# Hybrid RWKV-7 and attention block on one core: both levels of the block inverse on 32x32 tiles of TensorE, with strips of 64 columns for X and XT and the R and O products between their steps; final squares in two parts

## The chip, the core and the metric

The kernel runs on one core of a Trainium2 chip. The metric is the device time of one execution in microseconds (us); lower is better. PE is TensorE (PEld its weight loads), DVE is VectorE, ACT ScalarE, POOL GpSimd, and SP the engine whose queue starts the DMAs. T = 1024 tokens, model width 1024, all in float32 (F32R for the operands of the dense products).

## The reference, cut to what matters

One layer of a streaming encoder: norm, one input projection, an RWKV-7 head group (8 heads of 64) beside a sliding-window attention group, an output projection, a SwiGLU FFN, a final norm. The change touches the recurrence of the RWKV group and the final norm:

```python
def step(S, inp):
    r_t, w_t, k_t, v_t, kk_t, a_t = inp
    sa = jnp.einsum('bhvk,bhk->bhv', S, -kk_t)
    S = (S * w_t[:, :, None, :]
         + sa[..., None] * (kk_t * a_t)[:, :, None, :]
         + v_t[..., None] * k_t[:, :, None, :])
    return S, jnp.einsum('bhvk,bhk->bhv', S, r_t)
...
def rmsnorm(x, g):
    xf = x.astype(jnp.float32)
    y = xf * lax.rsqrt(jnp.mean(xf * xf, axis=-1, keepdims=True) + NORM_EPS)
    return (y * g.astype(jnp.float32)).astype(x.dtype)
```

## The kernel before, in words

The program is written out in eight stages; in each, every engine has a function of its own, and semaphores tie them together. Stages 1 to 3 (to 355 us) do the input projection, the attention and the inputs of the recurrence. Stage 5 (about 355 to 574 us) is the recurrence, stages 6 and 7 (to about 1082 us) are the output projection and the gate and up products, stage 8 is the down product and the final norm.

**The recurrence** takes the tokens in eight turns (`for t in range(NT)`) of 128. Within a turn the sequential rule is solved in matrices: for each of the 8 heads a 128x128 strictly triangular matrix (kept transposed in NB, two buffers by the parity of t), whose unit-triangular inverse is needed in its two 64x64 diagonal blocks. The inverse is made in three levels:

- `lanes(t)` on DVE (line 1613) inverts all 64 diagonal blocks of 16x16 (8 a head) with one partition for each. Its way in and out goes through DRAM: `gather` (1326) writes NB to `n_scratch` and reads the 16x16 blocks into LA; `scatter` (1340) writes the results (LM) to `inv_scratch` and reads them back as X (the inverse) and XT (its transpose), 128 partitions by 8 heads by 128 columns, with zeros where no block stands.
- Level 1 joins two blocks of 16 to one of 32, level 2 two of 32 to one of 64. On PE each level is `corners(n, t)` (NB times X, 1410) and `updates(n, t)` (the masked result Ts times XT, 1419), in two halves of four heads, each a product of 128x128 a head. DVE's `corners` (1599) multiplies by a mask of the constants and writes Ts1 or Ts2; DVE's `updates` (1607) adds the result to XT. Between the levels PE transposes XT (`transposed`, 1404) and ACT copies it to X.

**The order is written by hand.** Each engine runs its list in program order. PE in a turn: first corners, first updates, `outputs(t-1)` (transposes of the last turn's result, 1433), transposes for X, `cumulative(t+2)` (decay sums, 1254), second corners and updates, R (lines 1475 to 1480), the first part of O (1485), U, and the rest, ending in `following(t+1)`. DVE in a turn: corners, `normalise(t-1)` (1666), updates, `outputs(t-1)`, second corners and updates, `prepare(t+2)` (1291, four operations with ACT's exponentials of the decay sums), `lanes(t+1)`, masks of KB (1321), Sn (1720), means of the output, more masks of KB and, for turn t+2, of NB. ACT's exponentials (1277) come before its copy of R. PSUM has eight banks; `order5` (1221) lists the jobs in the order in which they take their banks, and a job waits for the one before it in its bank.

**The final norm** (stage 8): the last unit of the down product (m = 27) gives the block c21. `by_tokens` (2349) transposes it to tokens: its first three column blocks just before the unit's last two k steps, the fourth behind it. ACT squares 512 columns a token tile with a row sum (`square`, 2428); DVE adds the sums, ACT takes the root, both scale, and SP writes out.

## Time and profile before

| | |
|---|---|
| median of 3 runs | 1327.61 us (1326.69 to 1328.05) |
| profiled execution, its own time | 1324.93 us |
| its span, first to last instruction | 1323.0 us |
| granted TensorE clock, mean | 0.994 |
| busy: PE, PEld | 1275.8 us (96%), 1057.7 us (80%) |
| busy: DVE, ACT, POOL | 853.1 us (64%), 479.3 us (36%), 254.3 us (19%) |
| DMA | 179.05 MB, mean 135 GB/s |

The profiled execution is 2.7 us below the median. Busy times overlap and are averages over stages with different limits: the 96% of PE tell nothing of where a change on another engine would be felt. A matmul record ends when its result is out, so neighbouring records overlap; the distance between starts is what one costs in a stream.

### The profile page before, as it was taken

What the parts mean: (1) busy time and instruction counts of PE and PEld (TensorE: products, weight loads), DVE (VectorE), ACT (ScalarE), POOL (GpSimd) and SP (SyncE); (2) the same over time, 40 slices, a digit from 0 to 9 for tenths busy, and PEclk for the clock granted to TensorE, in tenths of its full rate; (3) what the DMA queues carried; (4) which work ended last, traced back from release to release, by engine and by line L of the source; (5) the groups of instructions that cost most, each with busy time, mean ns of one, the idle gap of its engine ahead of it and who ended that gap; (6) DMA issues with size and microseconds to landing.
All of it is one profiled execution on the core that took longest, in us unless ns stands there. A gap on an engine that the chain in (4) does not pass through costs nothing.

```text
span 1323.0 us, 18110 instructions
## 1 busy us (share of the span) xinstructions
PE 1275.8 (96%) x6973; PEld 1057.7 (80%) x6973; DVE 853.1 (64%) x1308; ACT 479.3 (36%) x847; POOL 254.3 (19%) x196
## 2 busy tenths in 40 slices
PE   7999999989899999999999999999999999999996
PEld 6888888655698888888878888888888888888885
DVE  6865623399778787744476656566777676546765
ACT  6100032488422232234363333333333334333334
POOL 0476600034300000000003331332233200000001
PEclk9999999999999999989999999999999999999998
DMA  5576532200322333333214123214544567766643
GB/s 222 173 246 232 207 121 92 104 2 17 80 71 71 75 103 94 115 123 127 80 48 127 52 93 96 83 62 159 175 141 162 191 222 293 250 210 209 210 140 135
DMA packets 117232, 179.05 MB, mean 135 GB/s; under 512 B 30368, under 2 KB 59040, under 8 KB 116896
## 3 DMA queue, kind: packets, MB, share of 16 engines
q1 hardware_dynamic: 117152, 177.96, 41.0%
q8 instruction: 53, 0.87, 0.3%
q14 instruction: 27, 0.22, 0.0%
HBM read 123.90 MB, written 53.49 MB: 134 GB/s over the span
## 4 chain that ended last, share of the span: by engine, by line
PE 88%; DVE 7%; issue 2%; DMA 2%; ACT 2%; POOL 0%; DVEq 0%; SPq 0%; ACTq 0%; POOLq 0%
PE bank L2317 28%; PE bank L369 21%; PE bank L2417 15%; PE bank L1400 4%; PE bank L474 2%; PE bank L383 2%; PE bank L1271 1%; PE bank L1527 1%; PE bank L1485 1%; PE bank L1479 1%; DVE scores L1178 1%; PE bank L992 1%; PE bank L1497 1%; PE bank L1514 1%; PE bank L1501 1%
## 5 line engine op out<-in xcount | busy, mean ns | idle before, releaser
L2317 PE MATMUL bank<-thi,ahi 128*128 128x512 f32 x320 | 124.5, 389 | 0.0
L2317 PE MATMUL bank<-tlo,ahi 128*128 128x512 f32 x320 | 124.5, 389 | 0.0
L2317 PE MATMUL bank<-thi,alo 128*128 128x512 f32 x320 | 124.5, 389 | 0.0
L2417 PE MATMUL bank<-ch,dwh 128*128 128x512 f32 x308 | 120.3, 391 | 0.6 <-DVE dwl L1995 0.6
L2417 PE MATMUL bank<-ch,dwl 128*128 128x512 f32 x308 | 119.9, 389 | 0.0
L2417 PE MATMUL bank<-cl,dwh 128*128 128x512 f32 x308 | 119.8, 389 | 0.0
L348 DVE TENSOR_TENSOR ring_wlo<-ring_raw,ring_whi 128x1024 fp32r<-128x1024 f32 x30 | 40.6, 1352 | 121.9 <-ACT ring_whi L342 121.9
L369 PE MATMUL bank<-hhi,ring_whi 128*128 128x512 f32 x288 | 114.4, 397 | 0.0
L369 PE MATMUL bank<-hhi,ring_wlo 128*128 128x512 f32 x288 | 112.2, 390 | 0.0
L369 PE MATMUL bank<-hlo,ring_whi 128*128 128x512 f32 x288 | 112.1, 389 | 0.0
L2317 PE MATMUL bank<-x1hi,ahi 128*128 128x512 f32 x240 | 93.4, 389 | 0.0
L2317 PE MATMUL bank<-x1lo,ahi 128*128 128x512 f32 x240 | 93.4, 389 | 0.0
L2317 PE MATMUL bank<-x1hi,alo 128*128 128x512 f32 x240 | 93.4, 389 | 0.0
L342 ACT ACTIVATE ring_whi<-ring_raw 128x1024 fp32r<-128x1024 f32 x30 | 31.6, 1057 | 153.8 <-PE bank L369 142.2
L1991 ACT ACTIVATE dwh<-dwr 128x1408 fp32r<-128x1408 f32 x28 | 38.7, 1382 | 112.7 <-PE bank L2417 108.1
L2317 PEld LDWEIGHTS bank<-thi,alo 128*128 128x128 f32 x320 | 60.1, 188 | 12.6
L2317 PEld LDWEIGHTS bank<-thi,ahi 128*128 128x128 f32 x320 | 60.1, 188 | 12.5
L2317 PEld LDWEIGHTS bank<-tlo,ahi 128*128 128x128 f32 x320 | 60.1, 188 | 12.4
L2417 PEld LDWEIGHTS bank<-ch,dwh 128*128 128x128 f32 x308 | 57.8, 188 | 12.9 <-DVE dwl L1995 1.0
L2417 PEld LDWEIGHTS bank<-ch,dwl 128*128 128x128 f32 x308 | 57.8, 188 | 12.1
L2417 PEld LDWEIGHTS bank<-cl,dwh 128*128 128x128 f32 x308 | 57.8, 188 | 11.8
L369 PEld LDWEIGHTS bank<-hhi,ring_whi 128*128 128x128 f32 x288 | 54.1, 188 | 11.9 <-issue 1.0
(336 smaller groups left out, 2862.2 us busy)
## 6 DMA issues: line engine op xcount, KB each, us to landing
hraw<-hid_scratch SPq DMA_DIRECT2D x12, 1024.0 KB, 5.7
hid_scratch<-hid SPq DMA_DIRECT2D x22, 512.0 KB, 6.1
hid_scratch<-rt SPq DMA_DIRECT2D x11, 1024.0 KB, 4.7
dwr<-down_sums SPq DMA_DIRECT2D x16, 704.0 KB, 4.2
ring_raw<-in_w_in SPq DMA_DIRECT2D x20, 512.0 KB, 4.3
raw_a<-in_w_gate_up SPq DMA_DIRECT2D x20, 512.0 KB, 4.4
raw_b<-in_w_gate_up SPq DMA_DIRECT2D x20, 512.0 KB, 5.2
dwr<-in_w_down SPq DMA_DIRECT2D x12, 704.0 KB, 4.1
```

The lines of the kernel that those rows point to most:

```text
L342: act.activation(self.ring.hi[:, s, 0:self.kt, :], self.ring.raw[:, s, 0:self.kt, :], ACT.Copy).then_inc(self.ring.hi_ready, 1)
L348: dve.tensor_tensor(self.ring.lo[:, s, 0:self.kt, :], self.ring.raw[:, s, 0:self.kt, :], self.ring.hi[:, s, 0:self.kt, :].bitcast(F32), AL ...
L369: mm = pe.matmul(o[:, :], wpart[:, s, k, :], apart[:, k, c], start=i == 0, stop=i == n - 1)
L383: mm = pe.matmul(bank[self.J.bank_of[f"{s}{half}"]][:, :], wpart[:, s, ks[n], :], apart[:, ks[n], c], start=n == 0 and i == 0, stop=n == l ...
L474: mm = pe.matmul(b[:, :], wpart[:, s, k, :], apart[:, k, c], start=k == 0 and i == 0, stop=k == KD - 1 and i == 2)
L992: mm = pe.matmul(bank[6][HD * e:HD * e + HD, p * P:(p + 1) * P], vt[:, t + j, (p // 2) * HD:(p // 2 + 1) * HD], pt[:, p % 2, j, e, :], sta ...
L1178: ins = dve.tensor_tensor_reduce(sc[:, h, c0:BAND], b[:, i * BAND + c0:(i + 1) * BAND], bias[:, h, c0:BAND], HD ** -0.5, snk[:, h:h + 1], ...
L1271: mm = pe.matmul(b[e][:, i * 2 * P:(i + 1) * 2 * P].rearrange("p (a n) -> p a n", a=2), src[r, 2 * g + i, tok(t)], rho_alpha(t, r, 2 * g + ...
L1400: mm = pe.matmul(b[:, j * P:(j + 1) * P], lhs(4 * g + j), rhs(4 * g + j), start=j == 0, stop=j == 3, skip_group_check=True)
L1991: act.activation(dw_hi[m % 2][:, :, :], dw_raw[m % 2][:, :, :], ACT.Copy).then_inc(ring2.hi_ready, 1)
L2317: mm = pe.matmul(b[:, :], w[:, k, :], m[:, k, :], start=opens and k == 0 and i == 0, stop=not (j, n) in parts and k == 3 and i == 2, skip_ ...
L2417: mm = pe.matmul(b[:, :], w[m % 2][:, k, :], a[:, k, :], start=opens and k == 0 and i == 0, stop=name not in PART2 and k == KF - 1 and i = ...
```

## The change

Per turn of the recurrence:

- Both levels of the inverse are computed on 32x32 tiles: `blocks_of` goes over the 8 heads and, for each, over four tiles (first corners with 16 columns, first updates with 32) or over two (the second level, and a new product for X that takes the place of the transposes). Each job fills one bank instead of two.
- X and XT keep 64 columns a head, the diagonal 64x64 blocks alone. Each is loaded in two transfers of 64 partitions, so that `scatter` issues five DMAs instead of three.
- On DVE the first corners are one `tensor_scalar` by a column of the constants, the first updates one add to X and one to XT, the last update two copies. ACT, which no longer copies X, copies Ts2.
- The order changes. On PE `outputs(t-1)` stands between the first corners and the first updates; the second corners stand behind R, the second updates behind O, and the decay sums for t+2 behind those. ACT takes its exponentials behind R and Ts2.
- The masks of the two levels (256 columns) leave the constants.

In stage 8 the first three column blocks of the last block are transposed two k steps earlier (at k = 7 instead of k = 9, of 0 to 10), ACT squares these 384 columns beside the last products, and only 128 columns a tile are left for the end; DVE adds the extra sums.

```diff
         for t in range(NT):
-            order5 += [("t10", t, 0), ("t11", t, 6), ("y10", t, 4), ("y11", t, 5)]
+            order5 += [("t1", t, 0), ("y1", t, 4), ("x1", t, 6)]
             order5 += [("ot", t - 1, 7)] if t else []
-            order5 += [("x10", t, 2), ("x11", t, 3)] + plan_cum(t + 2)
-            order5 += [("t20", t, 0), ("t21", t, 6), ("y20", t, 4), ("y21", t, 5)]
-            order5 += [("R", t, 0), ("O", t, 5), ("U", t, 2)]
+            order5 += [("R", t, 0), ("t2", t, 2), ("O", t, 5), ("y2", t, 4)] + plan_cum(t + 2) + [("U", t, 2)]
...
-                sp.dma_start(X[:, :, :], bass.AP(d_i.tensor, P, [[2 * P, P], [8 * IMG2, H], [1, P]])).then_inc(s_xl, 16)
-                if t:
-                    C.result(sp, "U", t - 1)
-                sp.dma_start(XT[:, :, :], bass.AP(d_i.tensor, 0, [[2 * P, P], [8 * IMG2, H], [1, P]])).then_inc(s_xt, 16)
+                for m, o, done in ((X, P, s_xl), (XT, 0, s_xt)):
+                    if t and m is XT:
+                        C.result(sp, "U", t - 1)
+                    for q in range(2):
+                        sp.dma_start(m[q * HD:(q + 1) * HD, :, :],
+                                     bass.AP(d_i.tensor, o + q * (2 * P + 1) * HD, [[2 * P, HD], [8 * IMG2, H], [1, HD]])
+                                     ).then_inc(done, 16)
...
+            def blocks_of(b, count, lhs, rhs, groups):
+                n = len(groups) * H
+                for h in range(H):
+                    for g in groups:
+                        lo, ro = lhs(g, h), rhs(g, h)
+                        to = g[2]
+                        mm = pe.matmul(b[32 * to:32 * to + 32, h * count:(h + 1) * count] if len(ro.shape) == 2 else
+                                       b[32 * to:32 * to + 32, h * count:(h + 1) * count].rearrange("p (a w) -> p a w", a=2),
+                                       lo, ro, start=h == 0, stop=h == H - 1, skip_group_check=True)
+                return mm
+            FOUR = [(g, g % 2, g) for g in range(4)]
             def corners(n, t):
+                if n == 1:
+                    b = C.claim(pe, "t1", t)
+                    pe.wait_ge(s_xl, 32 * t + 32)
+                    C.done(blocks_of(b, 16, lambda g, h: NB[t % 2][rows(g[0]), h, 1, rows(g[0])],
+                                     lambda g, h: X[rows(g[0]), h, 32 * g[1]:32 * g[1] + 16], FOUR), "t1", t)
+                else:
+                    b = C.claim(pe, "t2", t)
+                    C.emptied(pe, "x1", t)
+                    C.done(blocks_of(b, 32, lambda g, h: NB[t % 2][rows(g[0]), h, 1, rows(g[2])],
+                                     lambda g, h: X[rows(g[0]), h, 0:32], [(0, 0, 1), (2, 0, 3)]), "t2", t)
...
                 corners(1, t)
-                pe.wait_ge(s_xt, 16 * t + 16)
-                updates(1, t)
                 if t:
                     outputs(t - 1)
-                for g in range(2):
-                    C.emptied(pe, f"y1{g}", t)
-                    transposed("x1", g, t)
-                if t + 2 < NT:
-                    cumulative(pe, t + 2)
-                corners(2, t)
-                updates(2, t)
+                pe.wait_ge(s_xt, 32 * t + 32)
+                updates(1, t)
...
                 mm.then_inc(s_r, 1)
+                corners(2, t)
...
+                updates(2, t)
+                if t + 2 < NT:
+                    cumulative(pe, t + 2)
...
+            def first_corners(t):
+                b = C.result(dve, "t1", t)[:, 0:16 * H].rearrange("p (h n) -> p h n", h=H)
+                C.read(dve.tensor_scalar(Ts1[:, :, 0:16], b, cst[:, C_PAIR + 2:C_PAIR + 3], None, ALU.mult), "t1", t)
+            def first_updates(t):
...
+                C.read(dve.tensor_tensor(X[:, :, 0:16], c, X[:, :, 0:16], ALU.add), "x1", t)
+                C.read(dve.tensor_tensor(v, b, v, ALU.add), "y1", t)
+            def last_updates(t):
...
+                dve.tensor_copy(XT[0:32, :, 32:64], b[0:32, :, :])
+                C.read(dve.tensor_copy(XT[64:96, :, 32:64], b[64:96, :, :]), "y2", t)
...
-                    if m == 4 * len(TURN) - 1 and k == KF - 2:
+                    if m == 4 * len(TURN) - 1 and k == 7:
                         by_tokens(pe, 0, 1, 0, 3)
...
+            def square_three(n):
+                act.wait_ge(s_part, len(parts) + 12 + n + 1)
+                act.activation(fin[:, n, HALF:HALF + 3 * P], D2.bank("f01", n)[:, 0:3 * P], ACT.Square,
+                               accum_out=st[:, 4, n:n + 1]).then_inc(s_sq8, 1)
+            def square_last(n):
+                b = D2.result(act, "f01", n)
+                act.activation(fin[:, n, HALF + 3 * P:D], b[:, 3 * P:HALF], ACT.Square, accum_out=st[:, 1, n:n + 1]
+                               ).then_inc(s_sq8, 1)
```

How the order moves on PE in one middle turn. In these rows Ts_90 is Ts1 and Ts_91 is Ts2, `cst,sgt` are the decay sums, `S,arv` with the first `vtk,KB` is R, and the second `vtk,KB` is O. Before:

```order
L1400 MATMUL bank<-X,NB_89 128x128 x8
L1400 MATMUL bank<-XT,Ts_90 128x128 x8
L1437 MATMUL bank<-cst,on 128x128 x4
L1407 MATMUL bank<-cst,XT 128x128 x8
L1259 MATMUL bank<-cst,sgt 128x129 x4
L1400 MATMUL bank<-X,NB_89 128x128 x8
L1400 MATMUL bank<-XT,Ts_91 128x128 x8
L1476 MATMUL bank<-S,arv 128x128 x4
L1479 MATMUL bank<-vtk,KB 128x64 x8
L1485 MATMUL bank<-vtk,KB 128x64 x8
L1493 MATMUL bank<-rs,XT 64x64 x8
```

The same stretch of PE's list, from the first corners to U, in the changed kernel:

```order
L1406 MATMUL bank<-X,NB_89 32x16 x32
L1455 MATMUL bank<-cst,on 128x128 x4
L1406 MATMUL bank<-XT,Ts_90 32x32 x32
L1406 MATMUL bank<-Ts_90,XT 32x16 x16
L1487 MATMUL bank<-S,arv 128x128 x4
L1490 MATMUL bank<-vtk,KB 128x64 x8
L1406 MATMUL bank<-X,NB_89 32x32 x16
L1497 MATMUL bank<-vtk,KB 128x64 x8
L1406 MATMUL bank<-XT,Ts_91 32x32 x16
L1251 MATMUL bank<-cst,sgt 128x129 x4
L1507 MATMUL bank<-rs,XT 64x64 x8
```

The last update of the inverse (`XT,Ts_91`) has moved from ahead of R to behind O, and the decay sums from ahead of the second level to the last place before U.

On ACT, the same turn; `rs` is the copy of R, `ein` to `einv` the exponentials of the decay sums, which `prepare` on DVE reads. Before:

```order
L1547 ACTIVATE X<-bank 128x512 x2
L1284 ACTIVATE ein<-bank 128x258
L1285 ACTIVATE ecs<-bank 128x2
L1287 ACTIVATE ems<-bank 128x2
L1288 ACTIVATE einv<-bank 128x256
L1284 ACTIVATE ein<-bank 128x258
L1285 ACTIVATE ecs<-bank 128x2
L1287 ACTIVATE ems<-bank 128x2
L1288 ACTIVATE einv<-bank 128x256
L1570 ACTIVATE rs<-bank 64x512
L1572 ACTIVATE us<-bank 64x512
```

And in the changed kernel:

```order
L1576 ACTIVATE rs<-bank 64x512
L1561 ACTIVATE Ts_91<-bank 128x256
L1276 ACTIVATE ein<-bank 128x258
L1277 ACTIVATE ecs<-bank 128x2
L1279 ACTIVATE ems<-bank 128x2
L1280 ACTIVATE einv<-bank 128x256
L1276 ACTIVATE ein<-bank 128x258
L1277 ACTIVATE ecs<-bank 128x2
L1279 ACTIVATE ems<-bank 128x2
L1280 ACTIVATE einv<-bank 128x256
L1581 ACTIVATE us<-bank 64x512
```

The exponentials have moved behind the copy of R.

## Rows read from the trace of the kernel before

**Rows 1.** The page's fourth part: chain that ended last, shares of the span by engine.

```profile
PE 88%; DVE 7%; issue 2%; DMA 2%; ACT 2%; POOL 0%; DVEq 0%; SPq 0%; ACTq 0%; POOLq 0%
```

**Rows 2.** Chain of waits, whole span: start us, us, what.

```profile
468.33 1.16 PE bank L1400 x8
...
496.69 1.16 PE bank L1400 x8
```

**Rows 3.** Timeline of one turn, PE: start us, us, engine line op out<-in xcount [idle before].

```profile
466.98 1.13 PE L1400 MATMUL bank<-X,NB 128*128 128x128 f32 x8 [0.29 <-DMA X<-inv_scratch]
...
471.76 0.60 PE L1437 MATMUL bank<-cst,on 128*128 128x128 f32 x4
...
473.07 1.06 PE L1259 MATMUL bank<-cst,sgt 128*128 128x129 f32 x8
...
477.54 1.06 PE L1476 MATMUL bank<-S,arv 128*128 128x128 f32 x8
...
478.43 1.90 PE L1479 MATMUL bank<-vtk,KB 128*128 128x64 f32 x16
...
480.17 1.95 PE L1485 MATMUL bank<-vtk,KB 128*128 128x64 f32 x16
...
482.05 1.14 PE L1493 MATMUL bank<-rs,XT 64*64 64x64 f32 x16
...
495.26 1.02 PE L1400 MATMUL bank<-X,NB 128*128 128x128 f32 x7 [0.19 <-DMA X<-inv_scratch]
```

**Rows 4.** Timeline of the same turn, DVE, ACT and SP's queue.

```profile
466.94 2.56 DVE L1321 COPY_PREDICATED NB<-cst,bank 128x512 f32<-128x512 uint32 x4
...
470.06 0.67 DVE L1668 TENSOR_TENSOR on<-oc,sm 128x512 f32<-128x512 f32 x1
...
473.81 0.39 ACT L1284 ACTIVATE ein<-bank 128x258 f32<-128x258 f32 x1
...
474.81 0.48 ACT L1288 ACTIVATE einv<-bank 128x256 f32<-128x256 f32 x1
...
478.08 0.68 DVE L1297 TENSOR_TENSOR ab<-ab,einv 128x512 f32<-128x512 f32 x1
...
480.56 0.15 DVE L1640 TENSOR_TENSOR LM<-LA 64x8 f32<-64x8 f32 x1
...
487.80 0.58 SPq L1344 DMA_DIRECT2D inv_scratch<-LM  x1
...
488.71 1.35 DVE L1321 COPY_PREDICATED KB<-cst,bank 128x512 f32<-128x512 uint32 x2 [0.94 <-PE bank L1271]
...
491.09 0.38 SPq L1351 DMA_DIRECT2D X<-inv_scratch  x1
```

**Rows 5.** DMA issues in the recurrence: out<-in queue op xcount, KB each, median us to landing.

```profile
LA<-n_scratch SPq DMA_DIRECT2D x7, 64.0 KB, 2.7
```

**Rows 6.** Groups by line and shape, PE: busy us, mean ns of one, idle before.

```profile
L992 PE MATMUL bank<-pt,vt 128*64 128x128 f32 x256 | 21.3, 285 | 1.1
...
L1493 PE MATMUL bank<-rs,XT 64*64 64x64 f32 x128 | 9.1, 221 | 0.0
```

**Rows 7.** Timeline of the attention stage, PE.

```profile
328.45 0.66 PE L992 MATMUL bank<-pt,vt 128*64 128x128 f32 x8
```

**Rows 8.** Stretches: PE, PEld, DVE, ACT, POOL busy us, granted clock, DMA share, GB/s.

```profile
440.00:468.00 28.00, 27.29 (x252) 25.40 (x252) 21.94 (x49) 7.82 (x21) 1.46 (x3) 1.00 0.32 79
...
569.90:573.30 3.40, 2.85 (x14) 2.85 (x14) 1.78 (x2) 3.38 (x4) 0.00 (x0) 0.50 0.00 0
```

**Rows 9.** Timeline of the last turn, PE, around the drop of the clock.

```profile
568.63 1.14 PE L1514 MATMUL bank<-rs,XT 64*64 64x64 f32 x16 [0.68 <-ACT rs L1547]
...
570.46 3.67 PE L1527 MATMUL bank<-us,NB 128*128 128x64 f32 x16 [0.68 <-ACT us L1547]
```

**Rows 10.** Timeline of the last turn's head (DVE) and of the kernel's end (ACT).

```profile
553.81 0.69 DVE L1668 TENSOR_TENSOR on<-oc,sm 128x512 f32<-128x512 f32 x1 [1.49 <-POOL sm L1395]
...
1312.83 0.60 ACT L2431 ACTIVATE fin<-bank 128x512 f32<-128x512 f32 x1 [7.23 <-PE bank L2355]
```

More of the change, by code:

```diff
@@ L58, in constants @@
     c[:, C_LID:C_LID + 256:17] = 1
-    def corner(b):
-        return (s // (2 * b) == t // (2 * b)) & (s % (2 * b) >= b) & (t % (2 * b) < b)
-    for n, b in enumerate(LEVELS):
-        c[:, C_LEV + n * P:C_LEV + (n + 1) * P] = corner(b)
     c[:, C_BLK:C_BLK + P] = s // HD == t // HD
@@ L1419, in updates @@
-            def updates(n, t):
-                m = Ts1 if n == 1 else Ts2
-                for g in range(2):
-                    C.emptied(pe, f"t{n}{g}", t)
-                    b = C.claim(pe, f"y{n}{g}", t)
-                    C.done(four(b, g, lambda h: m[:, h, :], lambda h: XT[:, h, :]), f"y{n}{g}", t)
+            def blocks_of(b, count, lhs, rhs, groups):
[8 more added lines that the diff above has]
+                return mm
@@ new lines, in updates @@
+            def updates(n, t):
+                C.emptied(pe, f"t{n}", t)
+                if n == 1:
+                    b = C.claim(pe, "y1", t)
+                    C.done(blocks_of(b, 32, lambda g, h: Ts1[rows(g[0]), h, :],
+                                     lambda g, h: XT[rows(g[0]), h, :].rearrange("p (a w) -> p a w", a=2)[:, :, 16:32], FOUR),
+                           "y1", t)
+                    b = C.claim(pe, "x1", t)
+                    C.done(blocks_of(b, 16, lambda g, h: XT[rows(g[0]), h, 0:32],
+                                     lambda g, h: Ts1[rows(g[0]), h, 0:16], [(0, 0, 0), (2, 0, 2)]), "x1", t)
+                else:
+                    C.emptied(pe, "y1", t)
+                    b = C.claim(pe, "y2", t)
+                    C.done(blocks_of(b, 32, lambda g, h: Ts2[rows(g[0]), h, :],
+                                     lambda g, h: XT[rows(g[0]), h, 32:64], [(1, 0, 0), (3, 0, 2)]), "y2", t)
@@ L1513, in stage5_tensor @@
                 for h in range(H):
[L1514 removed]
+                    mm = pe.matmul(bu[high, h * HD:(h + 1) * HD], XT[high, h, :], rs_[high, h * HD:(h + 1) * HD],
                                    start=h == 0, stop=h == H - 1, skip_group_check=True)
@@ L1543, in stage5_scalar, with keep @@
             low, high = slice(0, HD), slice(HD, P)
-            def keep(job, t, dst, rows=slice(0, P)):
+            def keep(job, t, dst, rows=slice(0, P), cols=HALF):
                 b = C.result(act, job, t)
-                C.read(act.activation(dst, b[rows, :], ACT.Copy), job, t)
-            def keep_x(job, t):
-                for g in range(2):
-                    keep(f"{job}{g}", t, row(X[:, 4 * g:4 * g + 4, :]))
+                C.read(act.activation(dst, b[rows, 0:cols], ACT.Copy), job, t)
             def tokens(t):
@@ L1561, in stage5_scalar @@
                     mix_high(act, 0)
-                keep_x("x1", t)
-                if last:
+                    C.result(act, "x1", t)
                     mix_high(act, 1)
-                if t + 2 < NT:
-                    exponentials(act, t + 2, 0, 1)
-                if last:
                     mix_high(act, 2)
@@ L1570, in stage5_scalar @@
                 act.activation(rs_[low, :], bank[0][low, :], ACT.Copy).then_inc(s_rlow, 1)
+                keep("t2", t, row(Ts2[:, :, :]), cols=32 * H)
+                if t + 2 < NT:
+                    exponentials(act, t + 2, 0, 1)
                 act.wait_ge(s_u, t + 1)
@@ L1692, in stage5_vector @@
                 last = t == NT - 1
-                corners(1, t)
+                first_corners(t)
                 if t:
                     normalise(t - 1)
-                updates(1, t)
+                first_updates(t)
                 if t:
@@ L1700, in stage5_vector @@
                     mix_low(dve, 0)
-                corners(2, t)
-                if last:
                     mix_low(dve, 1)
-                updates(2, t)
+                last_updates(t)
                 if not last:
@@ L2353, in by_tokens @@
                 b = D2.bank(f"f{half}{g}", n) if first else D2.claim(pe, f"f{half}{g}", n)
+                if first:
+                    pe.wait_ge(s_sq8, 12 + n + 1)
                 for q in range(first, end):
@@ L2459, in stage8_scalar @@
                     first_columns(0)
+                    for n in range(4):
+                        square_three(n)
             for n in range(3):
-                square(0, 1, n)
+                square_last(n)
             root(1)
-            square(0, 1, 3)
+            square_last(3)
             first_columns(1)
@@ L2557, in stage8_vector @@
                 combine(m)
+            dve.wait_ge(s_sq8, 16)
+            order(dve.tensor_tensor(st[:, 0, 0:4], st[:, 0, 0:4], st[:, 4, 0:4], ALU.add))
             total(1)
```

59 lines of the change are left out of this document (19 added, 40 removed).

## The prediction

> **What bounds the kernel now.** I read first the chain of waits over the whole span: PE carries 88% of it [rows 1], most of it in dense products that the change leaves alone. The change lies in the recurrence (stage 5, about 355 to 574 us) and in the last 15 us. In the recurrence the same group of the chain comes back at 468.33 and 496.69 [rows 2]: a turn takes 28.36 us, and seven such steps separate the eight turns. A reader could stop here and call PE the bound, since it is busy 27.29 of 28.00 us there [rows 8]. But the timeline shows what PE waits for at the head of a turn: the last thing before the first corner products is the landing of X, with 0.29 us idle at 466.98 and 0.19 at 495.26 [rows 3]. Following X back through the timeline of the other engines [rows 4] gives a ring as long as the turn:
>
> - head (466.98) to the start of `prepare` on DVE (478.08): 11.10 us. DVE stands in program order: `prepare` follows the last update of XT.
> - `prepare` to the start of `lanes` (480.56): 2.48 us.
> - `lanes` to the issue of the scatter (487.80): 7.24 us.
> - scatter to the issue of X (491.09): 3.29 us; X to the next head (495.26): 4.17 us.
>
> The sum is 28.28 us. So two bounds lie on each other: PE's own work and the ring head, last update, `prepare`, `lanes`, scatter, X. Less work on PE is worth nothing unless "head to `prepare`" becomes shorter as well.
>
> **The change, part by part.**
>
> *Products of the inverse.* A turn loses 40 products of 128x128, which the trace counts as 80 instructions (two for each), and gains 112 products on 32x32 tiles, 224 instructions. The old price is 111 ns for an instruction: the 8 of L1476 start at 477.54 and L1479 follows at 478.43 [rows 3]. The new one is in no row, so I bound it. One 64x64 tile at a time: 16 instructions in 1.14 us, one lasting 0.221, so (1.14-0.221)/15 = 61 ns [rows 3, 6]; with half the columns 31 ns, the upper end. If two independent tiles overlap fully, the rate doubles: L992 alternates two column tiles and does 8 instructions of 128 columns in 0.66 us, (0.66-0.285)/7 = 54 ns, half of 111 [rows 6, 7]. Four tiles would make 31/4 = 8 ns, the lower end. Of the 224, 128 go to four tiles and 96 to two: (128x8+96x16)/224 = 11 ns. I take 13, near the lower end, because the row that is nearest shows full overlap: 2.9 us a turn instead of 8.9, between 1.8 and 6.9.
>
> *Changes of tile shape.* Each of the four tile groups now stands between wide products, also new. The nearest rows are wide to 64x64 and back: L1485 starts at 480.17, its 16 instructions at 111 ns end at 481.95 and L1493 starts at 482.05, 0.1 us later [rows 3]. I take 0.2 to 0.3 us for there and back, 1.1 us a turn. The Trainium skill (TensorEngine Tiling (Array Packing), Key Properties) says that changing the tiling mode drains the engine, and these 0.1 us agree.
>
> *The instruction floor.* The same page (Instruction Overhead) says that each matmul has some 60 cycles of overhead, so that one of a few columns costs as much as one of 60. By that page a step would be an estimated 25 ns, 5.6 us a turn, and the sum below would be about 22 us higher. It speaks against this change, and is a rival below, priced from rows.
>
> *The order on PE.* This is what I weigh most. Before, the second corners and updates ran ahead of R, and the decay sums for t+2 (L1259) ran early, so that ACT's exponentials were done at 475.29, long before `prepare` [rows 4]. Now the last update comes behind R and O, and the sums behind that, and behind those ACT's exponentials. Head to `prepare`, with 13 ns an instruction:
> corners 64x13 + 0.2 = 1.0; DVE's Ts1 and two handovers 0.6; DVE's `normalise` 0.67 and its handover 0.15, since `outputs` now stands ahead of the first updates on PE and waits for it [rows 4]: 2.4. `outputs`, 4 instructions (L1437) at 0.11 [rows 3]: 2.8. First updates 96x13 + 0.3: 4.4. R, 477.54 to 480.17, 2.6 [rows 3]: 7.0. Second corners 32x13 + 0.3: 7.7. O, 480.17 to 482.05, 1.9: 9.6. Second updates 0.7: 10.3. Decay sums and exponentials, 473.07 to 475.29, 2.2 [rows 3, 4]: 12.6 us, against 11.1. DVE's last update and ACT's copy of Ts2 cost nothing: they lie beside the sums and beside O.
>
> *X in strips.* X goes from one transfer of 512 KB (4.17 us) to two of 128 KB. Bounds: LA's 64 KB takes 2.7 us [rows 5], and nothing excludes that two issues and 256-byte pieces eat the gain. I take 3.6, so -0.5 a turn. XT has four issues' time more on SP, but is needed only after `outputs`.
>
> *The rest of the ring* (`prepare` on, 17.2 us) is unchanged. So a turn is longer by 1.5-0.5 = 1.0 us, seven times: +7. DVE loses eight and gains five short operations, but it was late nowhere in the ring; its tail behind `lanes` (masks, Sn, the head's means, masks; L1321 at 488.71 waits 0.94 us today [rows 4]) takes up the wait and ends about when X lands. PE then waits some 4 us for DVE's Sn, which frees the bank of `kt`: late next, and hidden under the ring.
>
> *Last turn.* No ring follows it, so here PE's saving counts: 80x0.111 = 8.9 less 2.9 and 1.1 is 4.9, of which the wait for POOL's power before `normalise`, 1.49 us [rows 10], stays: -3.3. Together +3.7 us at full clock.
>
> *Clock.* The profile shows the granted clock at 1.00 (2.4 GHz) through the whole recurrence but for one place: at 569.9 to 573.3 it is 0.50 (1.2 GHz) [rows 8]. What PE did just before was 64x64 products (L1514) with a wait of 0.68 us on either side, nothing wide [rows 9]; 16 instructions of L1527 then took 3.67 us, where 16 of the same shape take 1.90 (L1479) [rows 3, 9]. In the changed turn PE does, around the head, a wait, small tiles, a wait for `normalise`, four wide instructions and small tiles again: over 5 us with less wide work than before that drop. I expect the drop there in most turns. R follows: 24 instructions at (3.67-1.90)/16 = 0.11 us more each are +2.6 us on the ring. In 6 of 8 turns: +15.7 us.
>
> *Split squares.* Three fourths of the columns of four squares move under the last products. Of each of ACT's squares of 0.60 us on the last stretch [rows 10] about 0.25 goes, three of them on the path: -0.8 (between -1.1 and 0). The shorter constants load no later than before; I cost them at nothing, under the input's own loads.
>
> **The sum.** 3.7 + 15.7 - 0.8 = +18.6 us on the profiled execution's 1324.93 us: 1343.5. The median of the runs, 1327.61, is 2.7 above that execution, so I say 1346.
>
> **Rivals.**
>
> 1. *Small tiles are dearer*: one tile at a time, 31 ns, or a floor for each instruction. For it: no row shows four tiles or 16 columns. Against it: L992's full overlap. 31-13 = 18 ns on 224 instructions is 4.0 us a turn, 32 in eight: 1378; with the clock kept 1362; at half that excess with the drop 1362.
>
> 2. *The clock holds*, the pace as I take it. For it: a turn of today keeps 1.00 with three groups of 64x64 products and the waits at its head in it [rows 8]. 1346-15.7 = 1330.
>
> 3. *Faster*: the clock holds and four tiles run side by side at 8 ns. Place: the first updates behind `normalise`. 160 instructions on the ring 5 ns cheaper are -0.8 a turn, which with the strips of X landing in 3.1 us makes the turn 28.1 and the sum of the seven about -2, the last turn -4.4, the squares -0.8: 1320 to 1324. It decides when head to `prepare` falls below 11.1 us plus what X gains; at 13 ns it is 1.0 us over.
>
> **How the numbers follow.** Forecast (tiles near 8 to 16 ns, clock drops) 0.43, 1335 to 1355. Rival 1 0.27, 1355 to 1380. Rival 2 0.13, 1327 to 1334, half of it within 0.2%. Rival 3 0.14. An unseen slack in the ring that favours the change 0.03. About 0.2% (2.7 us) is what a measurement of this kernel can tell from no change. Faster 0.17, same 0.08, slower 0.75. The range leaves out the fast end of rival 3 and the dear end of rival 1: 1322 to 1374.
>
> **What would show it.** Right: turns of 30 to 32 us; `prepare` starting 12.5 us or more after the head, released by ACT's exponentials and not by the last update; `outputs` on PE waiting for `normalise`; granted clock 0.50 in most turns with R at twice its length; a new wait of PE for Sn. Wrong: small tiles over 20 ns an instruction in a stream (rival 1), PEclk 1.00 throughout (rival 2), or turns under 28.4 us, in which case the ring was not the bound that I make it.

## The result, and the profile after

The changed kernel takes 1406.05 us (median of 4 runs, 1390.90 to 1413.21) beside 1327.36 of the kernel before: 1.0555 times as long, interval 1.0472 to 1.0637. That is 79 us more, where I forecast 19. A ratio leaves out runs far above a kernel's fastest, so that of a kernel with a wide spread lies below the ratio of its medians. The profiled execution took 1413.21 us, the slowest of the four and 88.3 more than that of before; the rows below are its own.

Nearly the whole loss lies in the recurrence: from the first corners of turn 0 to the output projection it takes 306.6 us (354.20 to 660.81) instead of 219.2 (354.76 to 573.93), 87.4 of the 88.3 more. The page's clock line shows where to look:

```profile
PEclk9999999999655555555999999999999999999998
```

The stretches view of a middle turn, and of its parts at either clock (columns as in [rows 8]):

```profile
470.10:511.03 40.93, 37.83 (x406) 34.37 (x404) 20.87 (x47) 7.32 (x20) 1.83 (x2) 0.58 0.19 45
...
474.44:508.58 34.14, 34.14 (x318) 31.43 (x318) 15.68 (x37) 6.11 (x18) 0.00 (x0) 0.50 0.19 41
508.58:515.40 6.82, 3.72 (x92) 2.94 (x88) 5.19 (x9) 1.21 (x3) 1.83 (x2) 1.00 0.18 65
```

A turn is 40.93 us where it was 28.36 [rows 2], and for 34.14 of them the granted clock is 0.50 (1.2 GHz), with PE busy in all 34.14. In before it was 1.00 (2.4 GHz) throughout such a turn [rows 8]. PE's timeline of the same turn, to be held against [rows 3]:

```profile
476.32 2.08 PE L1487 MATMUL bank<-S,arv 128*128 128x128 f32 x8
478.18 3.51 PE L1490 MATMUL bank<-vtk,KB 128*128 128x64 f32 x16
481.63 1.06 PE L1406 MATMUL bank<-X,NB 32*32 32x32 f32 x32
482.62 3.67 PE L1497 MATMUL bank<-vtk,KB 128*128 128x64 f32 x16
486.23 1.06 PE L1406 MATMUL bank<-XT,Ts 32*32 32x32 f32 x32
487.22 2.09 PE L1251 MATMUL bank<-cst,sgt 128*128 128x129 f32 x8
...
511.03 0.73 PE L1406 MATMUL bank<-X,NB 32*32 32x16 f32 x64
514.86 0.63 PE L1455 MATMUL bank<-cst,on 128*128 128x128 f32 x4 [3.10 <-DVE on L1674]
```

R takes 5.31 us (476.32 to 481.63) instead of 2.63. The small tiles are not what is dear: the second corners take 0.99 us (481.63 to 482.62) and the second updates as much. The one wait left at the head is 3.10 us for `normalise`; it lies inside the stretch at 1.00, and the clock falls right behind it. DVE and ACT in that turn, beside [rows 4]:

```profile
489.73 0.40 ACT L1280 ACTIVATE einv<-bank 128x256 f32<-128x256 f32 x1
490.25 0.69 DVE L1289 TENSOR_TENSOR ab<-ab,einv 128x512 f32<-128x512 f32 x1 [2.06 <-ACT einv L1280]
...
511.35 2.53 DVE L1313 COPY_PREDICATED NB<-cst,bank 128x512 f32<-128x512 uint32 x4
513.78 0.34 DVE L1605 TENSOR_SCALAR Ts<-bank,cst 128x128 f32<-128x128 f32 x1
514.03 0.68 DVE L1674 TENSOR_TENSOR on<-oc,sm 128x512 f32<-128x512 f32 x1
```

As forecast, ACT's exponentials now release `prepare`. `normalise` is late because Ts1 and it stand behind DVE's masks of NB, which end 2.85 us after the head (511.03 to 513.88); the prediction had put their end at about the landing of X. `outputs` starts 3.83 us after the head, where its list has 2.4.

### The profile page after: what moved, and what is told of

Read it like the earlier page. It is cut to its first block, busy times and chain, and to the rows that moved or that the text cites. A ratio compares the mean times of both kernels' runs of the same rounds, so it can differ in the third digit from the quotient of the medians.

```text
span 1411.3 us, 20489 instructions
## 1 busy us (share of the span) xinstructions
PE 1345.7 (95%) x8189; PEld 1117.1 (79%) x8189; DVE 841.3 (60%) x1285; ACT 475.5 (34%) x847; POOL 254.0 (18%) x196
## 4 chain that ended last, share of the span: by engine, by line
PE 86%; DVE 7%; DMA 3%; ACT 2%; issue 2%; SPq 0%; POOL 0%; DVEq 0%; ACTq 0%; POOLq 0%
PE bank L2321 26%; PE bank L363 19%; PE bank L2425 13%; PE bank L1406 2%; PE bank L1497 2%; PE bank L1490 2%; PE bank L1263 2%; PE bank L468 2%; PE bank L377 2%; PE bank L1541 2%; DVE NB L1313 1%; PE bank L1511 1%; PE bank L1528 1%; PE bank L1507 1%; PE bank L1487 1%
## 5 line engine op out<-in xcount | busy, mean ns | idle before, releaser
L363 PEld LDWEIGHTS bank<-hlo,ring_whi 128*128 128x128 f32 x288 | 54.1, 188 | 12.0 <-issue 1.0
```

Of the source, the lines that this page charges most:

```text
L363: mm = pe.matmul(o[:, :], wpart[:, s, k, :], apart[:, k, c], start=i == 0, stop=i == n - 1)
```

## The experiments

All kernels, in the order of their runs; each ratio is to the kernel before as it ran beside them, with medians of 1325.6 to 1326.5. The last two columns are one stretch of the profiled execution, from the first R to the output projection, and its granted clock; for the changed kernel 303.3 us at 0.59, for the kernel before 209.9 at 0.99.

| kernel | median us (range) | ratio (interval) | stretch us | clock |
|---|---|---|---|---|
| squares | 1325.97 (1324.2-1328.1) | 0.9995 (0.9984-1.0007) | 209.9 | 1.00 |
| outputs back | 1368.97 (1364.5-1376.4) | 1.0322 (1.0273-1.0370) | 260.1 | 0.72 |
| fill | 1358.07 (1343.2-1370.0) | 1.0167 (1.0115-1.0219) | 250.7 | 0.80 |
| old order | 1384.35 (1375.8-1387.5) | 1.0417 (1.0377-1.0457) | 273.3 | 0.64 |
| fill three | 1358.86 (1345.5-1363.2) | 1.0218 (1.0164-1.0272) | 254.4 | 0.81 |
| lanes first | 1395.59 (1394.0-1409.1) | 1.0561 (1.0507-1.0616) | 286.3 | 0.61 |
| lanes, strips | 1334.01 (1321.3-1359.3) | 1.0036 (1.0005-1.0067) | 224.0 | 0.80 |
| wide, outputs | 1336.71 (1334.7-1339.8) | 1.0089 (1.0070-1.0107) | 221.2 | 0.98 |
| reordered | 1355.18 (1353.5-1361.5) | 1.0217 (1.0200-1.0233) | 246.3 | 0.72 |
| reordered, fill | 1353.72 (1349.5-1361.2) | 1.0213 (1.0186-1.0240) | 243.1 | 0.75 |
| corners on ACT | 1334.31 (1319.3-1355.1) | 1.0020 (0.9988-1.0052) | 222.9 | 0.80 |
| strips, fill | 1316.60 (1313.8-1323.3) | 0.9930 (0.9908-0.9952) | 209.0 | 0.89 |
| corners on ACT, fill | 1320.08 (1312.8-1343.7) | 0.9914 (0.9894-0.9934) | 212.1 | 0.89 |
| fill elsewhere | 1330.24 (1327.0-1348.4) | 1.0056 (1.0024-1.0089) | 220.1 | 0.86 |
| fewer products | 1309.73 (1307.8-1312.9) | 0.9873 (0.9851-0.9894) | 196.7 | 0.92 |
| last turns | 1316.90 (1305.7-1321.3) | 0.9894 (0.9858-0.9931) | 213.7 | 0.90 |

**Squares**: the kernel before with the hunks of stage 8 from the diff above, and nothing else.

> The kernel before with the change of the last stage alone (three fourths of four squares beside the last products). My term for it was -0.8 us, between -1.1 and 0: 1326.5 against 1327.4. If the squares are part of the loss, this kernel is slower than before by a microsecond or more. The recurrence must read as before: turns of 28.4 us, granted clock 1.00.

The end is shorter: from the last transposes to the last scaling 3.57 us (1316.16 to 1319.73) instead of 4.61 (1312.46 to 1317.07). Of the total, -0.7 us stays within its uncertainty. The squares are no part of the loss.

**Outputs back**, the changed kernel with one job of PE moved:

```diff
                 corners(1, t)
-                if t:
-                    outputs(t - 1)
                 pe.wait_ge(s_xt, 32 * t + 32)
                 updates(1, t)
+                if t:
+                    outputs(t - 1)
```

> The changed kernel with the transposes of the last turn's result put back behind the first updates, so that PE goes from the first corners to the first updates with DVE's Ts1 alone between them. Theory A (the granted clock falls because PE has next to nothing wide to do at the head of a turn: small tiles and a wait): the wait for normalise is only moved by 160 small instructions, so the clock still falls and the time stays at 1390 to 1410. Theory B (it is that one wait of 3.1 us between first corners and first updates on the way to the ring's last update): with it gone the clock holds in most turns and the time comes to 1330 to 1350.

Neither number: 37 us came back, and the clock still fell in every turn, for 3.4 to 7 us at a time in most and for 37 and 68 us twice. The wait matters but is not the whole cause. With `outputs` moved PE waits elsewhere, 3.3 us for Sn among others.

**Fill**, the changed kernel with products that nobody reads, each into a bank that the next job overwrites:

```diff
+            def filler(b, count):
+                for i in range(count):
+                    pe.transpose(b[:, i % 4 * P:i % 4 * P + P], ident, ident)
...
                     b = C.claim(pe, "t1", t)
+                    filler(b, 12 if t else 0)
...
                 b = C.claim(pe, "ot", t)
+                filler(b, 8 if t < NT - 1 else 0)
```

> The changed kernel with 20 extra transposes of 128x128 a turn, whose result nobody reads: 12 ahead of the wait for X and 8 ahead of the wait for normalise, about 4.4 us of PE at 2.4 GHz. It adds work and takes none away. Theory A (waits and small tiles at the head let the granted clock fall, and the low clock is the whole loss): granted clock 1.00 through the recurrence, turns of 28 to 31 us, 1325 to 1350 us. Theory C (the small tiles themselves cost more than an instruction of their size, or lower the clock whatever stands beside them): the clock still falls in every turn, turns of 41 us or more, 1400 to 1440 us.

More work made it 48 us faster, and its granted clock is 0.80 where the changed kernel has 0.59: most of the loss is the clock's. In the trace a transpose is one instruction; the first 12 took 1.46 us (457.55 to 459.01), so that 20 add some 2.4 us a turn and not the 4.4 that I gave. The later expectations price them too dear in the same way. It missed my 1350 by 8 us, and the timeline of PE (then one row of DVE) shows why:

```profile
451.66 1.12 PE L1453 MATMUL bank<-cst,arv 128*128 128x128 f32 x4 [3.31 <-DVE Sn L1730]
...
457.55 1.53 PE L1418 MATMUL bank<-cst 128*128 128x128 f32 x12
459.01 0.73 PE L1406 MATMUL bank<-X,NB 32*32 32x16 f32 x64
459.67 1.09 PE L1418 MATMUL bank<-cst 128*128 128x128 f32 x8
...
461.39 0.72 PE L1406 MATMUL bank<-XT,Ts 32*32 32x32 f32 x62
461.94 0.18 PE L1406 MATMUL bank<-Ts,XT 32*32 32x16 f32 x1
...
462.55 1.27 PE L1493 MATMUL bank<-S,arv 128*128 128x128 f32 x8
...
470.99 0.69 DVE L1289 TENSOR_TENSOR ab<-ab,einv 128x512 f32<-128x512 f32 x1 [1.37 <-ACT einv L1280]
```

Its stretches:

```profile
450.08:456.90 6.82, 5.24 (x24) 4.14 (x26) 5.04 (x11) 3.00 (x7) 0.00 (x0) 0.50 0.45 87
456.90:480.80 23.90, 22.60 (x404) 20.18 (x400) 15.41 (x37) 4.23 (x13) 1.83 (x2) 1.00 0.19 52
```

The head now keeps 1.00. In five of the turns the clock falls at the wait of 3.31 us for Sn, which I had named as late next, or just behind it.

**Old order**: small tiles kept, the order of before.

```diff
                 updates(1, t)
+                if t:
+                    outputs(t - 1)
+                if t + 2 < NT:
+                    cumulative(pe, t + 2)
+                corners(2, t)
+                updates(2, t)
...
                 mm.then_inc(s_r, 1)
-                corners(2, t)
```

> The changed kernel's small tiles in the order of before: outputs, decay sums, second corners and second updates ahead of R, exponentials ahead of the copy of R. Theory A: all 224 small instructions and their handovers to DVE and ACT now stand together at the head, with still less wide work between them, so the clock falls as before in every turn: 1385 to 1415. If the new order is what costs (theory D), the clock holds, turns are 26 to 28.5 us and the time 1310 to 1330.

One us under theory A's range, and far from D. Putting the order back does not put the time back. This kernel has no wait for `normalise` at its head; it waits up to 2.5 us for Ts1 instead.

**Fill three**: the fill also ahead of the wait for Sn.

```diff
                     b = C.claim(pe, kind, t)
+                    filler(b, 14 if kind == "bt" and t else 0)
```

> With 20 extra transposes the clock still fell for 6.8 us of every turn, right behind a wait of 3.3 us of PE for DVE's Sn. This kernel has extra transposes ahead of all three waits: 14 ahead of the kt transposes that wait for Sn, 8 ahead of X, 8 ahead of normalise, about 6.7 us of extra PE work a turn. Theory A (each stretch of waiting or of small tiles lets the clock fall, wherever in the turn it stands): granted clock 1.00 through the middle turns, turns of 29 to 30.5 us, set by the ring through DVE, 1330 to 1345 us. Theory C (the small tiles lower the clock whatever stands beside them): it falls in every turn as before, 1358 us or more.

The median missed theory A's range and is the number that I gave for theory C, but the clock did not fall in every turn as C has it: one of five middle turns has 27 us at 0.50, the other four hold 1.00 and take 29.0 to 30.3 us, as expected. The shortest of them:

```profile
424.30:453.30 29.00, 26.41 (x437) 23.60 (x436) 20.72 (x47) 7.22 (x20) 1.83 (x2) 1.00 0.26 62
```

In the next turn PE stands for 1.05 us within the first updates, with no releaser in the profile, and the clock is then 0.50 for 27 us. A turn of this order at full clock, with the fill in its waits, is thus 29.0 to 30.3 us: the order, the tiles and the strips together cost 0.6 to 1.9 us a turn, and the other 10.6 to 11.9 of the changed kernel's 40.93 are the clock's.

**Lanes first**, to take waits away instead of filling them: `lanes(t+1)` ahead of `prepare(t+2)`, and ACT instead of DVE copies the last update.

```diff
-                last_updates(t)
...
-                    if t + 2 < NT:
-                        prepare(dve, t + 2)
                     lanes(t + 1)
+                    if t + 2 < NT:
+                        prepare(dve, t + 2)
```

> The changed kernel with lanes(t+1) ahead of prepare(t+2) on DVE, and the last update of XT copied by ACT, so that DVE needs nothing of PE between outputs(t-1) and prepare. No extra work. The waits of PE for Sn (3.3 us) and for X should go, only that for normalise stays. Theory A: with less waiting PE keeps its clock in most turns, turns of 26.5 to 29 us, 1310 to 1335 us. If the one wait for normalise beside the small tiles of the head is enough for the clock to fall, it is low again in most turns: 1370 to 1400 us.

The second branch: with the 3.10 us for `normalise` left, the ratio (1.0561) is that of the changed kernel.

**Lanes, strips**: that, with `outputs` back as above, and the following (three changes at once, so their shares are not known):

```diff
-                sp.dma_start(bass.AP(d_n.tensor, 0, [[P, P], [8 * IMG, H], [1, P]]), NB[t % 2][:, :, 1, :]
-                             ).then_inc(s_img, 16)
+                for q in range(2):
+                    sp.dma_start(bass.AP(d_n.tensor, q * (P + 1) * HD, [[P, HD], [8 * IMG, H], [1, HD]]),
+                                 NB[t % 2][q * HD:(q + 1) * HD, :, 1, q * HD:(q + 1) * HD]).then_inc(s_img, 16)
```

> As the kernel with lanes first, and with outputs(t-1) behind the first updates on PE and n_scratch written from the 64 columns of each head's diagonal blocks alone (two transfers of 128 KB in place of one of 512 KB), which brings LA forward by about 1.5 us. Of the turn's waits only that for Ts1 is left. Theory A: granted clock near 1.00, turns of 25 to 27.5 us, 1300 to 1325 us, faster than both kernels. Theory C: the clock falls all the same, 1350 us or more.

A middle turn, and the last one:

```profile
415.50:441.40 25.90, 22.62 (x406) 20.32 (x404) 20.37 (x46) 7.86 (x22) 1.84 (x2) 1.00 0.22 45
551.06:581.40 30.34, 25.92 (x342) 24.64 (x340) 10.54 (x14) 9.83 (x14) 1.83 (x2) 0.50 0.17 63
```

The turn of 25.90 us was hit; the time was not, because the clock fell for 27 us in turn 0 and for 51 from the end of turn 6. At three heads between it fell for 3.4 us only, at one for 7. The fastest of ten runs, 1321.3, already beats the kernel before.

**Wide, outputs**: the kernel before with `outputs(t - 1)` moved ahead of the first updates.

> The kernel before, wide products and all, with one move of the change: outputs(t-1) on PE between the first corners and the first updates. PE then waits about 2 to 2.6 us for normalise at the head of each turn, and the ring is longer by 0.7 to 1.5 us a turn: 1333 to 1338 us if the clock holds. Theory A in its simple form (a wait of that length at the head is enough) says that the clock falls in most turns too and the time is 1350 us or more; if it holds at 1.00, the wait alone is not enough and the missing wide work of the inverse is needed as well.

```profile
363.60:560.40 196.80, 181.99 (x1666) 166.80 (x1664) 146.59 (x327) 51.42 (x128) 12.87 (x14) 1.00 0.32 84
```

The clock holds although PE waits there (0.25, 0.26 and 1.40 us at one head); turns are 29.6 us, 1.2 more than before. Beside wide products waits of this length do no harm; the wait for `normalise` is 1.40 us here and 3.10 in the changed kernel, so that this run doesn't try a wait as long as that one.

**Reordered**, and the same with fill:

```diff
-            order5 += [("t1", t, 0), ("y1", t, 4), ("x1", t, 6)]
+            order5 += [("t1", t, 0), ("y1", t, 3), ("x1", t, 1)]
...
+                C.read(act.activation(Ts1[:, :, 0:16], b, ACT.Copy, scale=cst[:, C_PAIR + 2:C_PAIR + 3]), "t1", t)
...
+                if t + 2 < NT:
+                    cumulative(pe, t + 2)
                 pe.wait_ge(s_vtk, 16 * t + 16)
```

> The kernel with lanes first and strips, whose middle turns are 25.8 to 26.4 us at the full clock and wait 2.5 us for Ts1 behind DVE's masks of NB. Here ACT makes Ts1, y1 and x1 take banks that the masks do not hold, the decay sums stand within R so that prepare runs while DVE waits for LA, and vtk is loaded ahead of XT. No extra work. Theory A: the last long wait of PE in a middle turn is gone, turns of 24 to 25.5 us with the granted clock at 1.00, 1295 to 1320 us, the rest lost where the clock falls in the first and last turns. Theory C (small tiles lower the clock by themselves): a drop in most turns, 1330 us or more.

> The same kernel with extra transposes in the waits that are left: 8 ahead of the first updates of turn 0, 2 in middle turns, 6 in the last turn and 3 ahead of each of its three waits for ACT. At most 31 transposes, about 6.9 us of PE, nearly all inside waits. Theory A: the clock also holds from turn 0 on and in the last turn: 1290 to 1305 us, and a narrower spread than the kernel without them. If the low clock of the first and last turns has another cause, the two kernels agree within their intervals or this one is 2 to 5 us slower.

Theory A missed by 35 us or more, twice; the first kernel's time and its drops are those that I gave for theory C. It is no clean test of C, because the edit made new waits: 0.5 to 1.3 us ahead of or within the first updates (1.5 us for XT once, with fill) and 0.9 us behind the second updates, which the decay sums no longer cover. The clock fell in each turn but the fill's first.

**Corners on ACT**: lanes and strips with the first two pieces of that diff only.

> The kernel with lanes first and strips, with Ts1 made by ACT and y1 and x1 in banks that DVE's masks do not hold, and nothing else of the reordered kernel (decay sums behind the second updates, vtk behind XT, as with strips). No extra work. The wait of 2.5 us at the head of a middle turn becomes 0.5 to 1 us, and the waits of 1.5 us for XT and of 0.9 us behind the second updates that the reordered kernel had do not appear. Theory A: turns of 24.8 to 25.8 us with the clock at 1.00 in most of them, 1300 to 1325 us. If the lower share of wide work in a turn that is shorter decides, and not the waits, the clock falls in most turns as in the reordered kernel: 1335 to 1360 us.

The median lies between the two branches. There are turns of 24.0 us at 1.00 (477.30 to 501.30), but one stretch of 34 us and one of 51 at 0.50. The runs spread over 36 us, with mean clocks from 0.975 (1319.3) to 0.943 (1355.1).

**Strips, fill**: lanes and strips with

```diff
                 if n == 1:
                     b = C.claim(pe, "y1", t)
+                    filler(b, 6 if t == 0 else 8 if t < NT - 1 else 6)
                 C.emptied(pe, f"t{n}", t)
```

and `filler(bank[1], 3)` ahead of the last turn's waits for ACT.

> The kernel with lanes first and strips, with extra transposes in its waits and no other change: 8 ahead of the first updates of a middle turn (1.8 us in a wait of 2.5), 6 in turn 0 and in the last, 3 ahead of each wait for ACT in the last. Nearly all lie inside waits, so at a full clock they cost under 5 us in all; the kernel without them had its middle turns at 25.8 to 26.4 us but the clock at 0.50 for 27 us of turn 0 and for 51 us from the end of turn 6. Theory A: the clock holds, 1298 to 1312 us, faster than both kernels. If the fall of the first and last turns does not come from the waits that are filled, 1325 to 1340 us, as without the fill.

Faster than both kernels, 5 us above what I expected. The timeline of a head:

```profile
407.31 0.73 PE L1407 MATMUL bank<-X,NB 32*32 32x16 f32 x64
408.49 1.06 PE L1431 MATMUL bank<-cst 128*128 128x128 f32 x8 [0.45 <-DVE NB L1313]
410.46 0.72 PE L1407 MATMUL bank<-XT,Ts 32*32 32x32 f32 x62 [0.91 <-DVE Ts L1621]
```

A turn with it, and the last:

```profile
381.78:407.31 25.53, 23.55 (x415) 21.23 (x413) 20.00 (x45) 7.86 (x22) 1.87 (x2) 1.00 0.31 76
...
543.42:570.70 27.28, 26.10 (x229) 24.10 (x218) 8.38 (x10) 8.45 (x12) 1.13 (x1) 0.50 0.13 48
```

**Corners on ACT, fill**: the same helper with 6, 3 and 8, and 4 behind the second updates of turns 6 and 7.

> The kernel with Ts1 made by ACT (turns of 24 us where the clock holds, but 1319 to 1355 us by its draws) with extra transposes in its waits: 3 at the head of a middle turn, 6 in turn 0, 8 in the last, 4 behind the second updates of the last two turns, where the decay sums are missing, and 3 ahead of each of the last turn's two later waits. Theory A: turns of 24 to 25 us at the full clock, 1300 to 1315 us, the fastest of all. If 3 transposes at the head are too few for the clock, 1320 to 1345 us, spread as before.

Between the two: five middle turns of 24.8 to 26.8 us (from R to R), one of 39.0 at the low clock.

**Fill elsewhere**:

```diff
-                    filler(b, 6 if t == 0 else 8 if t < NT - 1 else 6)
...
                 bo = C.claim(pe, "O", t)
+                filler(bo, 6 if t == 0 else 8 if t < NT - 1 else 6)
```

> The kernel that took 1316.6 us with the same number of extra transposes a turn, but those at the head (6, 8, 6) moved to stand between the second corners and O, where PE never waits: the head has its wait of 2.5 us whole again. If what counts is the wide work of a whole turn, the clock holds as with the fill in the waits and only the transposes' own 1.8 us on PE is added: 1318 to 1330 us. If what counts is the stretch at the head itself, the clock falls as in the kernel without fill: 1330 to 1355 us, with its wide spread.

```profile
465.47 0.71 PE L1407 MATMUL bank<-XT,Ts 32*32 32x32 f32 x62 [2.51 <-DVE Ts L1621]
...
466.83 1.11 PE L1461 MATMUL bank<-cst,on 128*128 128x128 f32 x4
467.74 1.91 PE L1493 MATMUL bank<-S,arv 128*128 128x128 f32 x8
```

Behind each head the clock is 0.50 for 3.4 us (R's first 8 instructions take 1.70 us to the next start instead of 0.89), but not for longer in the middle turns before the last of them. In the kernel with the same transposes in the waits it is 1.00 from 385 to 430 us, with such a head in it. Both theories are half right: where the wide work stands decides that the clock falls. How much of it follows may decide how soon the clock returns; no run shows that. The 8 transposes take 0.93 us there, not 1.8.

**Fewer products** (the kernel before; three of four heads' products of the inverse are left out, and DVE leaves XT as it is):

```diff
-                for j in range(4):
-                    mm = pe.matmul(b[:, j * P:(j + 1) * P], lhs(4 * g + j), rhs(4 * g + j), start=j == 0, stop=j == 3,
+                for j in range(1):
+                    mm = pe.matmul(b[:, j * P:(j + 1) * P], lhs(4 * g + j), rhs(4 * g + j), start=True, stop=True,
```

> The kernel before with three fourths of the inverse's wide products left out (30 of 40 a turn: one of four heads in each group is computed, and DVE's updates write XT unchanged); no 32x32 tile anywhere, order and DMAs as before. PE has 6.7 us less wide work a turn in a ring that does not get shorter by as much. If the missing wide work alone lets the clock fall, it falls in the middle turns here too: granted clock 0.50 for 50 us or more of the recurrence, 1330 to 1380 us. If the small tiles themselves are what lowers the clock, it holds at 1.00 and the time is 1300 to 1322 us.

```profile
432.16 0.46 PE L1400 MATMUL bank<-X,NB 128*128 128x128 f32 x2 [0.33 <-DMA X<-inv_scratch]
433.46 0.49 PE L1400 MATMUL bank<-X,NB 128*128 128x128 f32 x2 [0.84 <-DVE NB L1321]
435.03 0.77 PE L1400 MATMUL bank<-XT,Ts 128*128 128x128 f32 x4 [1.08 <-issue]
...
436.75 1.90 PE L1259 MATMUL bank<-cst,sgt 128*128 128x129 f32 x8
```

The clock falls at the head of nearly every middle turn, with no 32x32 tile in the kernel: products taken out of a head that waits are enough. The edit doesn't part less wide work from more waiting, for PE then waits longer for the same ring (20.2 us against 5.6 in all from 364 to 540 us). It was 0.50 for 3.4 us at a time there, 37 us in all instead of the 50 expected, and the total came out as for the other theory.

**Last turns**: strips and fill with 18 more transposes in the last two turns (5 behind the second updates, 11 at the last head, 6 ahead of `normalise`).

> The kernel that took 1316.6 us still had the clock at 0.50 for 44 us from the end of turn 6, where PE waits 0.9 us for the last update of XT, 1.6 us for Ts1 and 1.2 us for normalise. This one has 18 more extra transposes there: 5 behind the second updates of turns 6 and 7 (3 before, in turn 7 alone), 11 in place of 6 at the last head and 6 ahead of the wait for normalise. Theory A (short waits next to small tiles let the clock fall, filled waits keep it): 1300 to 1310 us. If the clock falls there for another reason, 1314 to 1322 us.

The median, 1316.9, lies in the second range, but the runs fall into two groups, one for each: 1305.7 to 1307.8 us in three runs, with mean clocks of 0.989 to 0.990, and 1316.9 to 1321.3 in four, with 0.978 to 0.979. The profiled execution is one of the four. It has one middle turn at full clock, and a next one that is not:

```profile
383.67:408.73 25.06, 23.55 (x412) 21.24 (x413) 19.98 (x45) 7.86 (x22) 1.84 (x2) 1.00 0.28 62
408.73:448.00 39.27, 38.80 (x412) 35.36 (x412) 19.36 (x43) 8.07 (x22) 1.59 (x2) 0.57 0.18 40
```

One turn at the low clock costs 14.2 us, about what parts the groups; that the three faster runs lack such a turn was not profiled. Of the kernels that compute everything this one has the lowest ratio to the kernel before, 0.9894 (0.9858 to 0.9931); its interval overlaps those of the other two with fill and strips.

## Why the prediction was wrong

**The step that failed is the clock term.** The prediction has "24 instructions at (3.67-1.90)/16 = 0.11 us more each are +2.6 us on the ring. In 6 of 8 turns: +15.7 us". R did take 2.68 us more, and the clock fell in every turn, but it stayed low for 34.14 us and not for R alone. At the full clock those 34.14 us would be an estimated 17.1 of work; with the 3.72 of the rest PE has 20.8 us of work a turn (the turn of lanes, strips at 1.00 has 22.62 busy), and so 6 to 8 us of slack in a ring of 29.0. The drop eats the slack and adds 10.6 to 11.9 us. The sum charges the low clock to R's 24 instructions alone, as if the drop ended there. The trace of before already spoke against that. The stretch of 0.50 that ends at 573.3 in [rows 8] goes on for as long again:

```profile
573.30:576.70 3.40, 3.40 (x11) 2.82 (x11) 2.29 (x5) 0.71 (x2) 0.00 (x0) 0.50 0.52 145
576.70:580.00 3.30, 3.30 (x16) 2.71 (x15) 1.66 (x2) 0.00 (x0) 2.49 (x2) 0.99 0.99 422
```

So that drop is 6.8 us long, with PE busy for 6.25 of them and from 573.93 us on in dense 512-column products. In the kernels here drops last 3.4 to 68 us. The term should have been "at half speed the turn is PE's own 41 us", and the range should have reached that far.

**The bound.** The ring was right as long as the clock held: head to `prepare` 11.98 us in the kernel with fill (459.01 to 470.99), forecast 12.6; a turn 29.0 to 30.3 with fill three, forecast 29.4. At the low clock it bounds nothing, since PE is busy in all 34.14 us of the low stretch, which I did not foresee.

**Small tiles.** Forecast 2.9 us and 1.1 for the changes of shape. Measured at full clock in the kernel with fill: first corners 64 instructions in 0.66 us (459.01 to 459.67), first updates 96 in 1.16 with their changes (461.39 to 462.55), second corners and second updates 0.63 each: 3.1 us for both terms. Four tiles do run side by side: in the first updates 62 instructions of 32 columns start within 0.55 us, 9 ns each, where the prediction has 31 for one tile at a time. On the other side it counts 80 instructions for the 40 wide products; 8 of them are transposes, which the trace counts once (`L1407`, x8). That makes 72, and from L1407's 0.87 us in before (472.20 to 473.07) some 8.0 us a turn instead of 8.9. The floor of the Trainium skill (TensorEngine Tiling (Array Packing), Instruction Overhead), an estimated 25 ns, does not show: the corners take 10 ns an instruction. Rival 1 (1378) came nearest in time, and by the wrong cause; its sign, over 20 ns an instruction, is not there (19.7 ns on two tiles with the change of shape, 10 and 12 on four).

**X in strips.** 2.8 us to landing and two issues 0.6 apart are 3.4, forecast 3.6. **Squares.** Forecast -0.8; the end became 1.04 us shorter. **Last turn.** The -3.3 cannot be seen; it ran at 0.53. **Sn.** The new wait shows where the clock holds: 3.31 us with fill, none in the changed kernel.

**The rivals.** Rival 2 (1330) fell with the clock; even with fill the recurrence is at 0.80. Rival 3 was not reached by this order: turns under 28.1 us of small tiles at full clock first stand in the kernel with `lanes` ahead of `prepare`, and strips, which I had not looked for.

**What stays open.** What makes a drop last 3.4 us or 34 (with outputs back, one of 68). Waits and the absence of wide work let it fall: fill at the head against fill elsewhere, and fewer products, show that. Small tiles are not needed for it. That they make a drop last longer would fit "fewer products" beside the changed kernel, but those two differ in more than the tiles, and with fill elsewhere the drops behind small tiles at the heads last 3.4 us too. Nor does a turn's work alone decide: in corners on ACT and in last turns the same list of work has turns at the full clock and turns with 34 us at the low one.

## What to carry to other kernels

Before small work takes the place of wide products on PE, look at what the granted clock is and ask what the stretch costs if all of it runs at 1.2 GHz: an engine with 6 to 8 us of slack in 29 has none then. If the clock falls, take the waits next to the small work away, and fill what is left with products nobody reads; here 8 transposes a turn in a wait of 2.5 us turned 1334.0 into 1316.6. Run such a kernel several times, and read the clock of each run before its time.

## What the runs showed of the hardware

- Unbroken work does not bring the clock back at once. In the changed kernel PE is busy in 34.14 of 34.14 us at 0.50, and its first 4.8 us of dense 512-column products in the output projection run at 0.50 too. The Trainium skill (TensorE: Matmul & The Clock Gate, HAM oscillation) tells of steps that start at the low clock after each wait, and this trace agrees; in its example the waits cost more than the low clock does, here a wait of 3.10 us has 34 us at the low clock behind it.
- Shorter waits are not always better. With one wait of 2.5 us a turn (lanes, strips) the stretch ran at 0.80, with several of 0.5 to 1.3 us (reordered) at 0.72; the two differ in the order of the work as well.
- One kernel has two groups of times some 12 us apart (last turns), with mean clocks of 0.978 and 0.989.
- The 64 instructions of 32 products with 16 columns, on four tiles, start within 0.66 us; 62 with 32 columns within 0.55 us.
